# Attention tiles every third step, and vector work moved to the steps that carry attention, in a two-layer encoder on one core

## The chip, the core and the metric

The kernel runs on one core of a Trainium2 chip. A core has five engines with their own instruction queues, which meet through semaphores: TensorE (PE, matrix products), VectorE (DVE), ScalarE (ACT), GpSimd (POOL) and SyncE (SP, which here only issues DMAs). Each engine works its queue strictly in order, so an instruction that waits holds up all that stand behind it. The metric is the device time of one run in microseconds (us), as the median of three.

## The reference

Two layers of a bidirectional encoder over 1024 tokens of width 1024, in float32. Layer 0 has windowed attention with 12 heads over 4 key/value heads; layer 1 has 12 heads, each with three groups of queries (dilations 1, 4 and 16) over the same keys, whose outputs are mixed by their softmax denominators. Both rotate the first 32 of 128 head dimensions, cross-attend with 4 heads into 256 memory tokens, gate, project and normalise.

```python
q, k, v, mq, gate = split_proj(einsum('bld,de->ble', x, w_in), SPLIT)
q, k = apply_rope(q, pos), apply_rope(k, pos)          # first 32 dims of each head
# layer 0: o = softmax over |t-s| <= 128 with a sink logit
# layer 1: for (window, dilation) in ((128,1), (512,4), (2048,16)):
#     o_g, lse_g = band_attention(dilate(q_g), dilate(k), dilate(v))
#   o = sum_g softmax(lse)_g * o_g
y = concat([o_mix, memory_attention(mq, mem, w_mkv)]) * silu(gate)
x = layer_norm(ALPHA * x + y @ w_out, ln_g, ln_b)
```

## The kernel before, in words

The order of all work is written out by hand on a clock of steps, which every engine's program walks through in the same way (`run(layer)` in each engine's block).

**Pairs and steps.** The input projection is done in pairs of 128 output columns: layer 0 has 20 pairs, layer 1 has 40. A pair costs 28 steps (`STEPS`), which are 7 half-size products (a Strassen-like scheme with 7 products in place of 8) of 4 steps each. A step is three matmuls, L1045, L1046 and L1047, of the weights split into a high and a low part. "Step 6 of a pair" below is its seventh step.

**Weights.** Each product takes one stage of weights. SP loads four raw quarters a pair; DVE forms four sums of quarters (`first_sum` to `fourth_sum`); ACT copies the high part (L1261) and DVE subtracts it for the low part (`split_lo`, at steps 2, 6, 10, ... three stages ahead). Nearly all two-operand DVE work goes through the helper `two` and so has the line L1505. The first, second and third sum are made right after `split_lo` of products 0, 1 and 3.

**Results of a pair.** ACT and DVE combine the products in PSUM (`summed`, L1584, on DVE at steps 16, 20 and 24). The one of step 24 (`c11_done`) is what product 0 of the next pair waits for, since it gets the bank.

**Rotary pass.** Each half (512 tokens) of a query or key takes four DVE instructions, one a step (`turn` L1599, `by_cosine`, `by_sine`, `turn_ends`), that start at the steps in `Pair.ropes`: 17 and 25, with two destinations also 21 and 29.

**Attention.** A `Job` is one head (layer 1: one group of a head) with 8 tiles of 128 queries. Tile n of a job that starts at T has its scores on PE at T+2n (L1095, into two banks in turn), its mask with the row minimum on DVE one step later (L1647), the exponential on ACT at +2 (L1339), in layer 0 the normalisation on DVE at +3 (L1653, L1657), the transposes on PE at +5 (L1109), their copy on ACT (L1322), the product with the values on PE at +7 (L1121), and ACT moves each finished half out at +8 (L1368, `output_half`). Scores of tile n wait for the mask of tile n-2, transposes for the exponential.

**Heads of layer 1.** Head i owns pairs 3i (queries of groups 0 and 1), 3i+1 (key and value) and 3i+2 (queries of group 2, and a gate). Its group 0 job runs in pair 3i+2, group 1 in pair 3i+3, group 2 in pair 3i+4, each from step 2. These three are called the g0, g1 and g2 stretches here; in a steady state the three follow each other 12 times. The mixing of head i is timed from T0, the start of pair 3i+5 (a g0 stretch): SP writes the softmax statistics to memory and reads them back token by token from step 0 (L852, L858), DVE works out weights at 11 and 14, SP broadcasts them at 16 to 18 and 29, and DVE multiplies and adds (`mix`, 5 instructions a half) at 26 to 30 and 35 to 39. Steps beyond 27 lie in the next pair, a g1 stretch. The gate product is L1626.

## Time and profile before

| | us |
|---|---|
| three runs | 2269.94, 2273.15, 2278.72; median 2273.15 |
| the profiled execution | 2270.71, span of its instructions 2268.9 |
| PE busy | 2151.3 (95%) |
| weight loads (PEld, beside PE), 11072 of them | 1805.3 (80%) |
| DVE busy | 1629.9 (72%) |
| ACT busy | 1145.5 (50%) |

PE is busy nearly all the time and sets the length; what is not useful in it is idle time and time at the lower of its two clock levels. DVE's 72% is a mean: its work is unevenly spread over the steps. Where matmuls are pipelined, the end of one is modelled, so what a wait costs is read more truly from the distance between starts than from the printed idle time.

### The profile page before, as it was taken

To read this page: it belongs to the slowest core of one execution; us is meant where nothing else is said; L and a number is where in the kernel's file an instruction comes from. 1 tells how busy PE (TensorE), PEld (TensorE's weight loads), DVE (VectorE), ACT (ScalarE), POOL (GpSimd) and SP (SyncE) were. 2 spreads that over 40 slices of the span, in tenths; PEclk is the share of its full clock that TensorE was granted. 3 is DMA by queue.
4 is the path that set the end of the run, shared out by engine and by line. 5 is a ranking of instruction groups with operands and counts; after the bars stand their busy time and mean duration, and the time that the engine had idled before them with its cause. 6 is when DMAs were issued, how large, how long until landed. Compare 5 with 4: busy or idle time off the path is not lost.

```text
span 2268.9 us, 32275 instructions
## 1 busy us (share of the span) xinstructions
PE 2151.3 (95%) x11072; PEld 1805.3 (80%) x11072; DVE 1629.9 (72%) x3673; ACT 1145.5 (50%) x2709; POOL 48.6 (2%) x65
## 2 busy tenths in 40 slices
PE   8999999999999977999999999999999999999996
PEld 8888887878887766887787878877888788888875
DVE  6777777777653759678777777787787777676375
ACT  5454545455543333555555655555556555565332
POOL 0000000000000210000000000000000000000021
PEclk9999999999999988999999999999999999999998
DMA  8311111111147441111212122122121121324743
GB/s 261 92 47 47 56 47 52 54 58 52 47 136 237 131 138 46 59 39 63 66 48 75 53 61 73 37 65 63 48 75 53 61 76 39 93 60 146 236 135 130
DMA packets 206796, 190.34 MB, mean 84 GB/s; under 512 B 20132, under 2 KB 160492, under 8 KB 206636
## 3 DMA queue, kind: packets, MB, share of 16 engines
q1 hardware_dynamic: 206636, 188.29, 26.9%
q8 instruction: 91, 1.49, 0.3%
q14 instruction: 69, 0.57, 0.1%
HBM read 160.01 MB, written 28.23 MB: 83 GB/s over the span
## 4 chain that ended last, share of the span: by engine, by line
PE 64%; DVE 27%; issue 5%; ACT 2%; DMA 2%; SPq 0%; DVEq 0%; ACTq 0%
PE bank L1045 11%; PE bank L1047 11%; PE bank L1046 11%; DVE work L1505 10%; PE bank L1095 7%; PE bank L1121 7%; DVE sums L1505 4%; PE bank L1215 4%; PE bank L1221 4%; PE bank L1109 4%; PE bank L1219 4%; DVE ring L1505 4%; DVE work L1584 2%; DVE work L1599 2%; DVE x_ops L1505 2%
## 5 line engine op out<-in xcount | busy, mean ns | idle before, releaser
L1045 PE MATMUL bank<-x_ops,ring 128*128 128x512 f32 (+1 forms) x1808 | 837.1, 463 | 29.9 <-issue 14.2
L1047 PE MATMUL bank<-x_ops,ring 128*128 128x512 f32 (+1 forms) x1808 | 702.4, 388 | 0.0
L1046 PE MATMUL bank<-x_ops,ring 128*128 128x512 f32 (+1 forms) x1808 | 700.3, 387 | 0.0
L1505 DVE SCALAR_TENSOR_TENSOR ring<-raw,ring 128x512 fp32r<-128x512 f32 x400 | 274.9, 689 | 413.5 <-ACT ring L1261 413.2
L1045 PEld LDWEIGHTS bank<-x_ops,ring 128*128 128x128 f32 x1808 | 347.8, 192 | 90.3 <-issue 43.6
L1047 PEld LDWEIGHTS bank<-x_ops,ring 128*128 128x128 f32 x1808 | 343.3, 190 | 71.6
L1046 PEld LDWEIGHTS bank<-x_ops,ring 128*128 128x128 f32 x1808 | 347.6, 192 | 43.9
L1322 ACT COPY work<-bank 128x256 f32<-128x256 f32 (+2 forms) x448 | 164.0, 366 | 405.2 <-PE bank L1109 403.9
L1261 ACT CAST ring<-raw 128x512 fp32r<-128x512 f32 x400 | 247.8, 621 | 201.1 <-PE bank L1221 172.3
L1095 PE MATMUL bank<-work 128*128 128x256 f32 (+2 forms) x896 | 270.1, 383 | 40.2 <-DVE soft L1647 40.2
L1121 PEld LDWEIGHTS bank<-work 128*128 128x128 f32 x1744 | 263.7, 191 | 43.9 <-ACT work L1368 4.4
L1339 ACT ACTIVATE work<-work,soft 128x256 f32<-128x256 f32 (+2 forms) x448 | 226.7, 506 | 126.1 <-DVE soft L1647 125.4
L1121 PE MATMUL bank<-work 128*128 128x128 f32 x1744 | 267.5, 275 | 3.4 <-ACT work L1368 1.9
L1095 PEld LDWEIGHTS bank<-work 128*128 128x128 f32 x896 | 181.9, 215 | 80.3 <-DVE soft L1647 49.7
L1505 DVE SCALAR_TENSOR_TENSOR work<-work 128x512 f32<-128x512 f32 (+4 forms) x352 | 232.6, 679 | 3.8
L1215 PE MATMUL bank<-ring,x_ops 128*128 128x512 f32 x512 | 200.5, 392 | 8.6 <-DVE x_ops L1505 7.2
L1505 DVE SCALAR_TENSOR_TENSOR work<-work,trig 32x512 f32<-32x512 f32 (+2 forms) x304 | 206.1, 708 | 0.0
L1221 PE MATMUL bank<-ring,x_ops 128*128 128x512 f32 x512 | 199.5, 390 | 0.0
L1219 PE MATMUL bank<-ring,x_ops 128*128 128x512 f32 x512 | 199.5, 390 | 0.0
L1109 PE MATMUL bank<-ident,work 128*128 128x128 f32 x872 | 170.7, 276 | 4.1 <-DVE work L1657 4.0
L1647 DVE CUSTOM_DVE_ANT_0 work<-bank,masks 128x256 f32<-128x256 f32 (+1 forms) x320 | 119.1, 377 | 64.2 <-PE bank L1095 63.0
L1505 DVE SCALAR_TENSOR_TENSOR ring<-sums,ring 128x512 fp32r<-128x512 f32 x180 | 121.0, 672 | 28.9 <-ACT ring L1261 28.9
(75 smaller groups left out, 2125.8 us busy)
## 6 DMA issues: line engine op xcount, KB each, us to landing
raw<-in_w_in_b SPq DMA_DIRECT2D x160, 256.0 KB, 3.0
raw<-in_w_out SPq DMA_DIRECT2D x128, 256.0 KB, 2.9
raw<-in_w_in_a SPq DMA_DIRECT2D x80, 256.0 KB, 3.0
work<-weight_scratch SPq DMA_DIRECT2D x24, 768.0 KB, 5.1
y_scratch<-work SPq DMA_DIRECT2D x32, 512.0 KB, 2.6
x_ops<-y_scratch SPq DMA_DIRECT2D x64, 256.0 KB, 3.8
raw<-in_w_mkv SPq DMA_DIRECT2D x32, 256.0 KB, 5.3
work<-in_x SPq DMA_DIRECT2D x4, 1024.0 KB, 8.1
```

What stands on the lines that cost most here:

```text
L1045: nc.tensor.matmul(dst, w_h, x_h, start=start, stop=False, skip_group_check=again)
L1046: nc.tensor.matmul(dst, w_h, x_l, start=False, stop=False, skip_group_check=again)
L1047: return nc.tensor.matmul(dst, w_l, x_h, start=False, stop=stop, skip_group_check=again)
L1095: nc.tensor.matmul(SB[count % 2][:, 0:size], q, k, start=True, stop=True).then_inc(s_ready, 1)
L1109: mm = nc.tensor.transpose(TB[x_n % 2][:, c * P:(c + 1) * P], p[:, k0:k0 + P], ident[:, :])
L1121: mm = nc.tensor.matmul(dst, job.values(v), pT[layer][count % 2][:, c * P:(c + 1) * P], start=(c == 0), stop=(c == len(chunks) - 1))
L1215: mm = nc.tensor.matmul(BB[b][:, :], y_h, ring[:, n % RING, 0, :], start=first, stop=False)
L1219: nc.tensor.matmul(BB[b][:, :], y_h, ring[:, n % RING, 1, :], start=False, stop=False)
L1221: mm = nc.tensor.matmul(BB[b][:, :], y_l, ring[:, n % RING, 0, :], start=False, stop=last)
L1261: nc.scalar.copy(ring[:, n % RING, 0, :], src).then_inc(w_hi, 1)
L1339: nc.scalar.activation(p_view(layer, count % 3, size, sink), s_view(layer, count % 3, size, sink), ACT.Exp, bias=low[:, job.stat, t:t + 1] ...
L1505: return nc.vector.scalar_tensor_tensor(out=dst, in0=a, scalar=1.0, in1=b, op0=ALU.mult, op1=op)
```

## The change

All of it is in the order of work; no arithmetic changes, and each engine gets the same instructions.

- The jobs of layer 0's 12 heads, and the group 0 and group 2 jobs of layer 1 (but for the last head's group 2), have a tile every third step (`gap=3`) in place of every second. A job then spans steps 2 to 31 of its pair's clock. The group 1 jobs and the memory jobs keep every second step.
- Rotary passes are listed pair by pair. Layer 1: the two queries of pair 3i go to steps 1 to 8 of pair 3i+1 and 1 to 8 of pair 3i+2; the key stays at 17 and 25; the group 2 query goes from 17 and 25 to steps 3 to 10 of the next pair. Layer 0: the keys go to steps 1 to 8 of the next pair, the queries stay.
- The first and third sum of weights are made at steps 3 and 15 of the pair before.
- Mixing is at 25, 27 to 30 and 39 to 43 (before 26 to 30 and 35 to 39), its statistics at step 27 (before 22); outputs, stores and one gate product move some steps later.
- The group 1 and 2 jobs' move-out waits for the mixing of the head before (`mixed`), no longer for its gated output.

```diff
-        ropes = [e for e in range(2) if self.dests[e].rope]
-        if ropes == [0]:
-            self.ropes = [(0, 1, 17), (0, 0, 25)]
-        elif ropes == [0, 1]:
-            self.ropes = [(0, 1, 17), (1, 1, 21), (0, 0, 25), (1, 0, 29)]
...
+        self.ropes = []
...
-            self.gates = [(1, 1, 21, 22), (1, 0, 29, 30)]
+            self.gates = [(1, 1, 21, 27), (1, 0, 29, 30)]
...
+        soon, later = [(0, 1, 17), (0, 0, 25)], [(0, 1, 29), (0, 0, 33)]
...
+            pairs[-1].ropes = later + [(1, 1, 57), (1, 0, 61)]
             add_pair(w_in_b[0], B_K + i * DH, Dest(b_k, "k", order=4), B_V + i * DH, Dest(b_v, "v"))
+            pairs[-1].ropes = soon
...
+            pairs[-1].ropes = [(0, 1, 31), (0, 0, 35)]
...
-            after = [(y_done, 2 * (NE + i))] if i else []
+            after = [(mixed, 10 * i)] if i else []
...
-                          stat=0, needs={0: [ready(pa, 0, 0), ready(pb, 0, 1)],
+                          stat=0, gap=3, needs={0: [ready(pa, 0, 0), ready(pb, 0, 1)],
...
+                          gap=3 if i < HEADS - 1 else 2,
...
-                n, odd = divmod(T - lag - job.start, 2)
+                n, odd = divmod(T - lag - job.start, job.gap)
...
-                if due is not None and due[1] in (0, 1, 3):
-                    {0: first_sum, 1: second_sum, 3: third_sum}[due[1]](due[0])
+                if due is not None and due[1] == 0 and due[0] in FIRST_PAIR:
+                    first_sum(due[0])
+                if due is not None and due[1] == 1:
+                    second_sum(due[0])
...
+                    for when, weight_sum in ((3, first_sum), (15, third_sum)):
...
-                            for h, first in ((0, 26), (1, 35)):
-                                if first <= s < first + 5:
-                                    mix(i, h, s - first)
+                            for h, times in ((0, (25, 27, 28, 29, 30)), (1, (39, 40, 41, 42, 43))):
+                                if s in times:
+                                    mix(i, h, times.index(s))
...
+                    third_sum(FIRST_PAIR[1])
                     fourth_sum(FIRST_PAIR[1])
```

**First place: DVE as a g1 stretch begins.** In both pieces the rows are DVE's from the `split_lo` of step 26 of the g0 stretch on; `ring` is a low part of weights, `raw` and `sums` are sums of weights, L1626 is the gate product and L1647 the mask of a tile (its second row reads out the minimum). Before:

```order
L1505 SCALAR_TENSOR_TENSOR ring<-sums,ring 128x512
L1505 SCALAR_TENSOR_TENSOR work<-work,trig 32x16x32
L1505 SCALAR_TENSOR_TENSOR work<-work 128x512
L1505 SCALAR_TENSOR_TENSOR work<-work,trig 32x512
L1505 SCALAR_TENSOR_TENSOR work<-work 128x512
L1505 SCALAR_TENSOR_TENSOR work<-work 32x16x32
L1505 SCALAR_TENSOR_TENSOR work<-work 128x512 x2
L1505 SCALAR_TENSOR_TENSOR ring<-sums,ring 128x512
L1505 SCALAR_TENSOR_TENSOR raw<-raw 128x512
L1505 SCALAR_TENSOR_TENSOR work<-work 128x512
L1626 SCALAR_TENSOR_TENSOR work<-work 128x512
L1647 ISA work,soft<-bank,masks 128x256
```

Now, from the same `split_lo` (L1517 is the helper's line, L1640 the gate product, L1661 the mask):

```order
L1517 SCALAR_TENSOR_TENSOR ring<-sums,ring 128x512
L1517 SCALAR_TENSOR_TENSOR work<-work 128x512
L1640 SCALAR_TENSOR_TENSOR work<-work 128x512
L1517 SCALAR_TENSOR_TENSOR work<-work 128x512 x2
L1517 SCALAR_TENSOR_TENSOR ring<-sums,ring 128x512
L1517 SCALAR_TENSOR_TENSOR work<-work 128x512
L1640 SCALAR_TENSOR_TENSOR work<-work 128x512
L1517 SCALAR_TENSOR_TENSOR sums<-raw 128x512
L1661 ISA work,soft<-bank,masks 128x256
```

The rotary rows (32 rows high) that stood among the mixing have gone behind the first mask, and a weight sum and a gate product have changed places with others.

**Second place: DVE in the later half of the g1 stretch.** From the `split_lo` of step 14; L1584 (now L1598) combines results of a product, L1599 (now L1613) begins a rotary pass. Before:

```order
L1505 SCALAR_TENSOR_TENSOR ring<-raw,ring 128x512
L1647 ISA work,soft<-bank,masks 128x256
L1647 ISA soft 128x1
L1584 SCALAR_TENSOR_TENSOR work<-bank,work 128x512
L1647 ISA work,soft<-bank,masks 128x256
L1647 ISA soft 128x1
L1599 STREAM_SHUFFLE work<-work 32x512
L1505 SCALAR_TENSOR_TENSOR ring<-raw,ring 128x512
L1505 SCALAR_TENSOR_TENSOR sums<-raw 128x512
L1505 SCALAR_TENSOR_TENSOR work<-work,trig 32x512 x2
L1584 SCALAR_TENSOR_TENSOR work<-bank,work 128x512
L1505 SCALAR_TENSOR_TENSOR work<-work 32x512
```

Now:

```order
L1517 SCALAR_TENSOR_TENSOR ring<-raw,ring 128x512
L1517 SCALAR_TENSOR_TENSOR work<-work 128x512
L1517 SCALAR_TENSOR_TENSOR raw<-raw 128x512
L1661 ISA work,soft<-bank,masks 128x256
L1661 ISA soft 128x1
L1517 SCALAR_TENSOR_TENSOR work<-work 128x512
L1598 SCALAR_TENSOR_TENSOR work<-bank,work 128x512
L1517 SCALAR_TENSOR_TENSOR work<-work 128x512
L1661 ISA work,soft<-bank,masks 128x256
L1661 ISA soft 128x1
L1517 SCALAR_TENSOR_TENSOR ring<-raw,ring 128x512
L1598 SCALAR_TENSOR_TENSOR work<-bank,work 128x512
```

The rotary passes are gone from here; two mixing rows, a weight sum and a gated output have come.

**Third place: PE in a g0 stretch,** two steps before and two after the change (L1109, now L1121, are transposes; L1121, now L1133, products with the values; L1095, now L1107, scores). Before:

```order
L1045 MATMUL bank<-x_ops,ring 128x512
L1046 MATMUL bank<-x_ops,ring 128x512
L1047 MATMUL bank<-x_ops,ring 128x512
L1121 MATMUL bank<-work 128x128 x2
L1109 MATMUL bank<-ident,work 128x128 x2
L1045 MATMUL bank<-x_ops,ring 128x512
L1046 MATMUL bank<-x_ops,ring 128x512
L1047 MATMUL bank<-x_ops,ring 128x512
L1095 MATMUL bank<-work 128x256
```

Now:

```order
L1057 MATMUL bank<-x_ops,ring 128x512
L1058 MATMUL bank<-x_ops,ring 128x512
L1059 MATMUL bank<-x_ops,ring 128x512
L1133 MATMUL bank<-work 128x128 x2
L1057 MATMUL bank<-x_ops,ring 128x512
L1058 MATMUL bank<-x_ops,ring 128x512
L1059 MATMUL bank<-x_ops,ring 128x512
L1121 MATMUL bank<-ident,work 128x128 x2
```

Value products and transposes of different tiles no longer share a step; the scores stand in a third one.

## Rows read from the trace of the kernel before

**Rows 1.** Waits of PE, 870 to 2050 us (total, times, longest).
```profile
PE bank L1095 <- DVE soft L1647: 40.2, 22, 3.0
```
**Rows 2.** By stretch: head 0's g1 stretch (layer 1, pair 3).
```profile
948.60:977.77 29.17, 28.43 (x149) 24.68 (x148) 19.35 (x45) 15.58 (x45) 0.00 (x0) 1.00 0.17 55
```
**Rows 3.** By stretch: two of the eleven other g1 stretches, and the sum of eleven.
```profile
1214.04:1247.97 33.93, 30.21 (x150) 25.69 (x149) 27.41 (x58) 16.39 (x46) 0.00 (x0) 0.95 0.23 71
...
1576.63:1609.26 32.63, 28.91 (x150) 24.77 (x149) 27.33 (x58) 16.52 (x46) 0.00 (x0) 1.00 0.24 73
...
sum 370.18, PE 329.76 PEld 280.60 DVE 297.44 ACT 180.63 POOL 0.31; mean PE 29.98 PEld 25.51 DVE 27.04 ACT 16.42 POOL 0.03
```
**Rows 4.** By stretch: sum of the eleven g2 stretches.
```profile
sum 289.20, PE 279.80 PEld 230.03 DVE 222.52 ACT 157.37 POOL 0.00; mean PE 25.44 PEld 20.91 DVE 20.23 ACT 14.31 POOL 0.00
```
**Rows 5.** PE in order of time, g2 stretch and next start (start, length, what [idle before]).
```profile
1246.83 0.39 PE L1047 MATMUL bank<-x_ops,ring 128*128 128x512 f32 x1
1247.97 0.47 PE L1045 MATMUL bank<-x_ops,ring 128*128 128x512 f32 x1 [0.75 <-DVE work L1584]
...
1253.98 0.40 PE L1047 MATMUL bank<-x_ops,ring 128*128 128x512 f32 x1
1255.07 0.49 PE L1095 MATMUL bank<-work 128*128 128x128 f32 x2 [0.68 <-DVE soft L1647]
...
1274.24 0.47 PE L1045 MATMUL bank<-x_ops,ring 128*128 128x512 f32 x1 [0.17 <-DVE work L1584]
```
**Rows 6.** DVE in order of time: rotary, four full rows, first mask of a g1 stretch.
```profile
1207.58 1.98 DVE L1505 SCALAR_TENSOR_TENSOR work<-work,trig 32x512 f32<-32x512 f32 x2
...
1217.71 2.48 DVE L1505 SCALAR_TENSOR_TENSOR work<-work 128x512 f32<-128x512 f32 x4
...
1222.52 0.41 DVE L1647 CUSTOM_DVE_ANT_0 work<-bank,masks 128x256 f32<-128x256 f32 x1
```
**Rows 7.** PE in order of time: steps with scores, with transposes, with value products.
```profile
1192.36 0.39 PE L1047 MATMUL bank<-x_ops,ring 128*128 128x512 f32 x1
...
1193.27 0.39 PE L1047 MATMUL bank<-x_ops,ring 128*128 128x512 f32 x1
...
1226.35 0.40 PE L1047 MATMUL bank<-x_ops,ring 128*128 128x512 f32 x1
...
1227.50 0.39 PE L1047 MATMUL bank<-x_ops,ring 128*128 128x512 f32 x1
...
1228.85 0.40 PE L1047 MATMUL bank<-x_ops,ring 128*128 128x512 f32 x1
...
1242.96 0.39 PE L1047 MATMUL bank<-x_ops,ring 128*128 128x512 f32 x1
...
1243.64 0.40 PE L1047 MATMUL bank<-x_ops,ring 128*128 128x512 f32 x1
...
1244.79 0.39 PE L1047 MATMUL bank<-x_ops,ring 128*128 128x512 f32 x1
```
**Rows 8.** The start of layer 1: its second pair, and PE's wait before it.
```profile
896.97:918.45 21.48, 21.17 (x85) 16.77 (x85) 18.33 (x42) 5.57 (x10) 0.00 (x0) 0.92 0.17 50
...
PE bank L1045 <- DVE work L1584: 2.2, 1, 2.2
```
**Rows 9.** Waits of PE and of weight loads in layer 0, 126 to 651 us.
```profile
PE bank L1109 <- DVE work L1657: 3.6, 9, 0.4
...
PEld bank L1109 <- DVE work L1657: 8.7, 12, 0.9
```
**Rows 10.** SP in order of time: exchange of softmax statistics, next weight loads.
```profile
1180.80 3.96 SPq L852 DMA_DIRECT2D soft_scratch<-work  x7
1185.85 2.68 SPq L858 DMA_DIRECT2D trig<-soft_scratch  x6
1192.35 0.94 SPq L776 DMA_DIRECT2D raw<-in_w_in_b  x2
```
**Rows 11.** ACT in order of time: a half of a group 1 job moved out.
```profile
1236.86 1.06 ACT L1368 COPY work<-bank 128x256 f32<-128x256 f32 x3
```

More of the change, by code:

```diff
@@ L163, in __init__ @@
     def __init__(self, start, tiles, order, values, out, group=0, sink=None, whole=True, stat=0,
-                 needs=()):
+                 needs=(), gap=2):
+        self.gap = gap
         self.start, self.tiles, self.order, self.values, self.out = start, tiles, order, values, out
@@ L371, in encoder @@
             add_pair(w_in_a[0], A_K + u * DH, k, A_V + u * DH, v)
+            pairs[-1].ropes = later
             for j in range(GROUP):
@@ L391, in encoder @@
                      b_col(1, i), Dest(b_q[1], "q", rot=4 * W_B))
+            pairs[-1].ropes = later + [(1, 1, 57), (1, 0, 61)]
             add_pair(w_in_b[0], B_K + i * DH, Dest(b_k, "k", order=4), B_V + i * DH, Dest(b_v, "v"))
+            pairs[-1].ropes = soon
             q = Dest(b_q[2], "q", order=16)
@@ L427, in encoder @@
                 for e, h, turn in pairs[g].ropes:
+                    assert T0 + turn not in ropes_at[layer]
                     ropes_at[layer][T0 + turn] = (g, e, h)
-                    rope_no[g, e, h] = len(rope_no)
                 for e, h, tanh, mul in pairs[g].gates:
@@ L432, in encoder @@
                     gate_no[g, e, h] = len(gate_no)
+            for T in sorted(ropes_at[layer]):
+                rope_no[ropes_at[layer][T]] = len(rope_no)
         def landed(g, e, h):
@@ L514, in encoder @@
                               order=A_ORDER, values=chunks_of(a_vbuf), out=a_o[j], sink=h,
-                              stat=h % 3,
+                              stat=h % 3, gap=3,
                               needs={0: [ready(gk, 0, 0), ready(gq, 0, 1)], 4: [ready(gq, 0, 0)]})
@@ L598, in encoder, with stat_time @@
         tile_no, x_no, y_no, job_no = {}, {}, {}, 0
-        stats_at = {step_at(1, 3 * i + 4, 22): i for i in range(HEADS)}
+        def stat_time(i):
+            return step_at(1, 3 * i + 4, 27 if i < HEADS - 1 else 22)
+        stats_at = {stat_time(i): i for i in range(HEADS)}
         y_at = ({}, {})
@@ L652, in x_of_tile @@
         def x_of_tile(layer, job, n):
-            return x_no[layer, job.start + 2 * n + LAG_T, "tile"]
+            return x_no[layer, job.start + job.gap * n + LAG_T, "tile"]
         def products(layer):
@@ L1766, in run @@
                         fourth_sum(pair.g + 1)
+                    for when, weight_sum in ((3, first_sum), (15, third_sum)):
+                        pair = pair_at(layer, T, when)
+                        if pair is not None and pair.g + 1 < FIRST_PAIR[layer] + PAIRS[layer]:
+                            weight_sum(pair.g + 1)
                     for job in jobs[layer]:
```

11 lines of the change are left out of this document (5 added, 6 removed).

## The prediction

> **What bounds the kernel now.** I read the page's busy shares first: PE 95%, DVE 72%, ACT 50%. PE sets the length, so only three things can move the time: how long PE stands, how long it runs at the lower clock level, and how its own instructions follow each other. Next I read who PE waits for. In layer 1's projection the scores wait 22 times for the mask on DVE [rows 1], twice for each of eleven heads. Then I laid windows on the pairs. A g1 stretch with nothing in its way takes 29.17 us; that is head 0's, which no mixing precedes [rows 2]. The eleven others take 32.6 to 34.2 us with the same matmuls, and the longer ones show a mean granted clock of 0.95, the shorter 1.00 [rows 3]. So behind a stand of some 3 us PE sometimes runs on at 1.2 GHz for a while. The window with the lower clock is 1.3 to 1.6 us longer than the one without.
>
> Last I read what DVE did before such a stand. In the stretch that begins at 1214.04 us, the first mask belongs to step 3 and starts at 1222.52, 8.5 us after the stretch began [rows 6]. DVE was never idle there: it was late, because steps 17 to 30 of the g0 stretch held two rotary passes, three combinations, weight sums, gate and mixing, while PE went through the steps after the last tile at only 0.68 us each (1242.96 to 1243.64) [rows 7]. A full-size DVE instruction costs 0.61 us (four in 2.48), a strided rotary product 0.99 (two in 1.98) [rows 6]. Each step without attention hides one DVE instruction, and these steps held more.
>
> **Prices on PE.** All prices are distances between starts of the third matmul of two steps [rows 7]: a bare step 0.68, with scores 1.15 (1226.35 to 1227.50), with value products and transposes together 1.35 (to 1228.85), with transposes alone 0.91 (1192.36 to 1193.27), with value products alone 1.15 (1243.64 to 1244.79).
>
> **Part 1: the g1 stretch.** Its tiles keep their spacing; what goes is the work ahead of them. I tallied DVE against PE from the start of the stretch. Up to the first mask DVE now has six full instructions (three mixing, one low part, one gate, one weight sum), 3.7 us; the mask needs the scores of step 2, which PE has done at 3.2. So the mask is done at about 4.1 us, against 8.9 before. Two strided rotary passes follow at steps 3 to 10, of 3.2 us each (begin and end 0.61, two products 0.99), among masks (0.35), low parts, output and the second mixing. By that tally masks 0 to 7 are done at 4.1, 6.4, 9.5, 11.6, 14.1, 15.7, 18.4 and 20.6 us. PE asks for the transposes of those tiles at 6.9, 9.0, 11.5, 14.0, 16.5, 19.0, 21.0 and 23.0. With 0.7 us for the exponential between, each is in time by 1.2 us or more. Hence no stand, and with it no lower clock. Gain: 370.18 - 11 x 29.17 = 49.3 us [rows 2, 3]. What is late next is ACT: at step 16 it waits for the last mixing instruction of step 15 (formerly for the output of step 12), done at some 19.0 us while PE enters step 16 at 17.7. Behind it in ACT's queue stand three copies of 1.06 us [rows 11] and the copy of transposed tile 5, which PE wants at 21. Between 0 and 1.3 us per head; I take 0.3, x 11 = 3 us lost.
>
> **Part 2: the g2 stretch.** Two stands, both visible as distances [rows 5]. At its first step, 1246.83 to 1247.97 is 1.14 where 0.23 is usual, so 0.91 lost: the combination of step 24 of the g1 stretch was late, behind rotary passes that are now elsewhere. At its first masks, 1253.98 to 1255.07 is 1.09, so 0.86 lost, for the pass that ran over from steps 25 and 29. Gain 11 x 1.77 = 19.5 us; the stretch's mean falls from 26.3 [rows 4] to 24.5. The new load here is the densest of the change: from step 16 to the combination of step 24, seven full instructions, one strided pass and two small masks make 8.1 us. PE wants that combination at step 28, at 24.5/28 = 0.88 us a step 10.5 us after step 16. It fits with 2.4 us to spare. DVE then enters the g0 stretch about 2 us late and has two more passes there, but now beside tiles; the tally has its first mask done at 5.2 us and PE asking for the transposes at 7.8.
>
> **Part 3: the g0 stretch.** The stand at its first step (0.17 idle shown, 0.33 by the same difference between shown and true as at the g2 start) has the same cause as the 0.91: 11 x 0.33 = 3.6 us. The end of this stretch, which made DVE late before, now holds 11 full instructions and four masks in steps 16 to 27, 8.1 us, over some 12 us of PE.
>
> **Part 4: the start of layer 1.** PE stands 2.2 to 2.4 us for the first pair's combination and then has a pair at clock 0.92 [rows 8]; seven of DVE's instructions ahead of that combination move off. I take 2.4 and 1.7 for the clock (0.08 of 21.48). Gain 4.1 us. Third sum of weights now before the last normalisations at the layer's end: one instruction, on the path there, costs 0.6.
>
> **Part 5: layer 0.** Transposes wait for DVE: 3.6 us idle on PE, 8.7 on the weight loads [rows 9]. These two bound it; with one instruction's start hidden under each I take 6.6 us. The rotary passes and tiles here tally at about DVE's full rate in steps 16 to 27 (14.7 us against 14.4), late by 1 us at most, which the four steps of slack hide.
>
> **Part 6: what PE pays.** 280 tiles (96 in layer 0, 96 + 88 in layer 1) now leave the product stream three times, not twice. Apart: 0.91 + 1.15 - 0.68 = 1.38; together 1.35 [rows 7]. The rows are rounded to 0.01, so 0.01 to 0.04 a tile, 3 to 11 us; I take 5.
>
> The Trainium skill ("TensorE: Matmul & The Clock Gate", section "Back-to-back issue gap") says that in a real stream the spacing of matmuls is set by weight load and matmul both, so that small matmuls leave a load uncovered. By that rule every new return to the product stream would show a load. These rows do not bear it out: the lone transposes add 0.23, barely over two of their starts. It stands below as a rival.
>
> **Parts with one answer.** Later outputs, stores and gates, and the memory jobs: nothing waits for them in the stretches above, the next reader of each buffer being a stretch or more away. If that cover went, each would cost its own 0.6 us once a head.
>
> **Sum,** against the profiled execution's 2270.71 (span 2268.9): 49.3 + 19.5 + 3.6 + 4.1 + 6.6 = 83.1 gained; 5 + 3 + 0.6 = 8.6 paid; 74.5 net, 2196.2. That execution lies 2.4 under the median 2273.15; I add 2 for that: 2198 us.
>
> **Rivals.**
> A. The backlog moves and does not go. For: DVE is near its full rate at the end of g2 and at the start of g1, with margins of 1.2 to 2.4 us, and one late semaphore uses them up. Against: the tallies. Price: 1.5 us in each of 12 heads and the full 1.3 on ACT in 11: 18 + 11 = 29 more: 2227.
> B. PE's switching. Every new return shows a whole weight load. For: the weight loads are busy 80% of the span. Against: [rows 7]. A load takes 0.163 us in the mean (1805.3 over 11072 loads, by the page): 280 x 0.163 = 46, 5 of it counted: 2239. This is the skill's rule above, as this kernel would show it.
> C. Slower. The statistics leave at step 27, not 22, so SP's exchange runs inside the g0 stretch. From its first write at 1180.80 to the last read issued at 1188.53 is 7.7 us, and 1.1 more if the reads land as the last write did (issued by 1184.76, waited out at 1185.85): 8.8 us [rows 10]. DVE needs it at step 11, at 29.17/28 = 1.04 us a step 11.5 us in, less half a step until the statistics are there: 2.2 us spare. If the exchange takes longer, DVE stands with all masks behind it, and SP's weight loads too. It decides from 75/12 = 6.2 us a head, an exchange of over 17 us; at 18 it gives 2280. For: the exchange will share the queues with weight loads. Against: nothing in the rows is nearly so slow.
> D. It does not do what it says: the waits put down to DVE are another's, and the time stays at 2270. Against: the 8.5 us without one idle moment on DVE.
>
> **How the numbers follow.** Forecast 0.78, A 0.13, B 0.03, C 0.03, D 0.03. 0.5% (11 us) is about what can be told from no change. Faster: forecast, A and B, 0.94; same: D, 0.03; slower: C, 0.03. Range: downward, nothing paid at ACT, 3 on PE and 8.7 in layer 0, then a few us for waits in the last heads that I left out: 2184. Upward, to A: 2226.
>
> **What would show it.** PE's waits for DVE at the scores go from 40.2 us to under 5; the eleven g1 stretches sum to 321 to 326, the g2 stretches to about 271; no clock below 1.00 between 910 us and the end of layer 1's projection; PE busy nearly unchanged in the g0 stretches. If part 1 is wrong, scores or transposes in g1 still wait for DVE, or value products for ACT at steps 17 to 21. If C holds, DVE waits for a DMA at its first copy of weights (L1671). The prediction is wrong if the product stream itself lengthens by over 0.05 us a tile.

## The result, and the profile after

The changed kernel takes 2181.57 us (median of four runs, 2181.03 to 2183.19) against 2271.55 us for the kernel before beside it: a ratio of 0.9598, 95% interval 0.9581 to 0.9616. The profiled execution took 2181.57 us, its span is 2179.8, which is 89.1 us under the span before. So the kernel is 4% faster, as forecast in sign and for the most part in cause, but the forecast of 2198 us was 16.4 us too high and the range ended 2.4 us above the result.

Of the page, first the busy shares, and then the first line on the chain of waits:

```profile
PE 2121.7 (97%) x11072; PEld 1787.8 (82%) x11072; DVE 1628.8 (75%) x3673; ACT 1139.9 (52%) x2709; POOL 48.6 (2%) x65
...
PE 91%; DVE 5%; issue 1%; DMA 1%; ACT 1%; SPq 0%; ACTq 0%; DVEq 0%
```

The chain of waits was 64% PE and 27% DVE before. DVE did the same work (1629.9 us before, 1628.8 after); only its times moved. PE's busy time fell by 29.6 us with the same matmuls.

The waits of PE from 860 to 1985 us (total, times, longest), which answer to [rows 1]:

```profile
PE bank L1133 <- ACT work L1334: 1.2, 2, 0.7
PE bank L1133 <- ACT work L1380: 0.7, 1, 0.7
PE bank L1121 <- DVE work L1671: 0.5, 1, 0.5
PE bank L1036 <- DVE x_ops L1517: 0.2, 1, 0.2
```

The 40.2 us at the scores (now L1107) are gone. By stretch, the windows that answer to [rows 3] (the same two heads, and the sum of the eleven g1 stretches), and to [rows 4] (sum of the g2 stretches):

```profile
1184.30:1213.50 29.20, 29.20 (x157) 25.51 (x156) 26.51 (x57) 16.84 (x47) 0.00 (x0) 1.00 0.25 82
...
1518.33:1547.56 29.23, 29.23 (x157) 25.52 (x156) 26.52 (x57) 16.84 (x47) 0.00 (x0) 1.00 0.25 82
...
sum 321.38, PE 321.38 PEld 280.67 DVE 291.65 ACT 185.20 POOL 0.31; mean PE 29.22 PEld 25.52 DVE 26.51 ACT 16.84 POOL 0.03
...
sum 269.79, PE 269.79 PEld 225.00 DVE 211.05 ACT 145.43 POOL 0.00; mean PE 24.53 PEld 20.45 DVE 19.19 ACT 13.22 POOL 0.00
```

PE is busy through the whole of each g1 window, at clock 1.00. At the g2 start, which answers to [rows 5], PE in order of time (start, length):

```profile
1213.28 0.39 PE L1059 MATMUL bank<-x_ops,ring 128*128 128x512 f32 x1
1213.50 0.39 PE L1057 MATMUL bank<-x_ops,ring 128*128 128x512 f32 x1
```

That is 0.22 between starts, where it was 1.14. And of DVE, for [rows 6], the low part of weights of step 26 and the first mask of the g1 stretch that began at 1184.30:

```profile
1184.15 0.69 DVE L1517 SCALAR_TENSOR_TENSOR ring<-sums,ring 128x512 fp32r<-128x512 f32 x1 [2.25 <-ACT ring L1273]
...
1189.58 0.42 DVE L1661 CUSTOM_DVE_ANT_0 work<-bank,masks 128x256 f32<-128x256 f32 x1
```

The mask starts 5.3 us into the stretch; before it was 8.5. The tally of the prediction had it done at 4.1, and it is done at about 5.7. DVE is not late by a backlog here: it stood idle for 2.25 us until ACT had copied the high part, and so began step 26's low part only as the stretch began. Nine full instructions, that one included, stand ahead of the mask, where the tally counted six.

The two layers as wholes, from the first matmul of the first pair to that of the last step. Before, then after (us, PE busy, weight loads, DVE, ACT, POOL, granted clock, DMA share, GB/s):

```profile
73.76:651.48 577.72, 572.61 (x2953) 473.82 (x2951) 420.28 (x1048) 286.93 (x676) 0.00 (x0) 1.00 0.17 54
856.85:2068.57 1211.72, 1153.74 (x6021) 974.18 (x6022) 926.53 (x2220) 682.55 (x1731) 0.31 (x1) 0.98 0.21 60
```

```profile
72.96:643.74 570.78, 570.30 (x2952) 471.58 (x2951) 420.72 (x1048) 283.92 (x676) 0.00 (x0) 1.00 0.18 55
849.03:1980.51 1131.48, 1127.11 (x6021) 959.36 (x6022) 924.37 (x2219) 679.78 (x1731) 0.31 (x1) 1.00 0.22 65
```

Layer 0 gained 6.9 us and layer 1 gained 80.2; the other 1.9 lie outside the projections, where the change moves nothing on PE.

### The profile page after: what moved, and what is told of

Its sections match the earlier page's. It is cut to its first block, busy times and chain, and to the rows that moved or that the text cites. A ratio compares the mean times of both kernels' runs of the same rounds, so it can differ in the third digit from the quotient of the medians.

```text
span 2179.8 us, 32275 instructions
## 1 busy us (share of the span) xinstructions
PE 2121.7 (97%) x11072; PEld 1787.8 (82%) x11072; DVE 1628.8 (75%) x3673; ACT 1139.9 (52%) x2709; POOL 48.6 (2%) x65
## 4 chain that ended last, share of the span: by engine, by line
PE 91%; DVE 5%; issue 1%; DMA 1%; ACT 1%; SPq 0%; ACTq 0%; DVEq 0%
PE bank L1059 18%; PE bank L1057 18%; PE bank L1058 18%; PE bank L1133 9%; PE bank L1107 9%; PE bank L1121 4%; PE bank L1227 4%; PE bank L1233 4%; PE bank L1231 4%; PE bank L1097 2%; DVE x_ops L1517 1%; DVE work L1517 1%; PE bank L1036 1%; DVE ring L1517 1%; DMA raw<-in_w_mkv 1%
## 5 line engine op out<-in xcount | busy, mean ns | idle before, releaser
L1058 PE MATMUL bank<-x_ops,ring 128*128 128x512 f32 (+1 forms) x1808 | 696.9, 385 | 0.0
L1517 DVE SCALAR_TENSOR_TENSOR ring<-raw,ring 128x512 fp32r<-128x512 f32 x400 | 273.0, 684 | 240.8 <-ACT ring L1273 240.6
L1058 PEld LDWEIGHTS bank<-x_ops,ring 128*128 128x128 f32 x1808 | 345.3, 191 | 36.5
L1133 PEld LDWEIGHTS bank<-work 128*128 128x128 f32 x1744 | 262.2, 190 | 44.5 <-ACT work L1334 3.7
L1133 PE MATMUL bank<-work 128*128 128x128 f32 x1744 | 267.3, 274 | 2.5 <-ACT work L1334 1.2
L1107 PE MATMUL bank<-work 128*128 128x256 f32 (+2 forms) x896 | 264.4, 376 | 0.0
L1517 DVE SCALAR_TENSOR_TENSOR work<-work 128x512 f32<-128x512 f32 (+4 forms) x352 | 233.3, 678 | 4.1 <-DMA work<-weight_scratch 0.9
L1517 DVE SCALAR_TENSOR_TENSOR ring<-sums,ring 128x512 fp32r<-128x512 f32 x180 | 123.1, 684 | 114.5 <-ACT ring L1273 114.5
L1517 DVE SCALAR_TENSOR_TENSOR work<-work,trig 32x512 f32<-32x512 f32 x304 | 207.1, 710 | 0.8
L1107 PEld LDWEIGHTS bank<-work 128*128 128x128 f32 x896 | 181.6, 215 | 30.2
L1121 PE MATMUL bank<-ident,work 128*128 128x128 f32 x872 | 168.2, 272 | 0.5 <-DVE work L1671 0.5
L1121 PEld LDWEIGHTS bank<-ident,work 128*128 128x128 f32 x872 | 114.4, 140 | 33.2 <-ACT work L1351 2.5
```

The lines of the kernel that those rows point to most:

```text
L1058: nc.tensor.matmul(dst, w_h, x_l, start=False, stop=False, skip_group_check=again)
L1107: nc.tensor.matmul(SB[count % 2][:, 0:size], q, k, start=True, stop=True).then_inc(s_ready, 1)
L1121: mm = nc.tensor.transpose(TB[x_n % 2][:, c * P:(c + 1) * P], p[:, k0:k0 + P], ident[:, :])
L1133: mm = nc.tensor.matmul(dst, job.values(v), pT[layer][count % 2][:, c * P:(c + 1) * P], start=(c == 0), stop=(c == len(chunks) - 1))
L1517: return nc.vector.scalar_tensor_tensor(out=dst, in0=a, scalar=1.0, in1=b, op0=ALU.mult, op1=op)
```

## The experiments

Each ran on the chip beside the kernel before; ratios are to that, with their 95% interval. "Changed kernel" is the kernel of the result, and edits are against that one unless said otherwise. A stand is a stretch of time in which PE waits. Line numbers shift by a few with some edits.

### 1. Rotary passes and weight sums at their old places (e1), rotary passes alone (e3)

```
 e3:      self.ropes = []           ->  passes at steps 17, 25 (and 21, 29)
          pairs[-1].ropes = later   ->  deleted, as the other four such lines
 e1: as e3, and first_sum and third_sum back at their old places
```

Both keep the new spacing, and also the new places of mixing, gates, statistics and outputs.

> The changed kernel with the rotary passes and the weight sums back at their old steps; tile spacing, mixing, gates and statistics stay at the new ones. Theory 1 (the gain comes from DVE work taken out of the steps ahead of a g1 stretch; spacing only makes room for it): about half of the 89 us is kept. The stand at the start of g2 (0.9) and at its masks (0.9) stays, the stand of 3.4 in g1 shrinks to about 2, the clock seldom falls: about 2225 us, 2215 to 2240. Rival 2 (the spacing alone gives the time, since it keeps PE slower and fed while DVE catches up): 2182 to 2190. Rival 3 (only the moves count): 2265 to 2275.

> The changed kernel with the rotary passes alone back at their old steps; the weight sums stay at 3 and 15. Theory 1: near the first experiment, better by the one weight sum (0.6 us) that no longer stands ahead of the first mask of g1 and one in steps 17 to 24: 2210 to 2225. Rival 2: 2182 to 2190. If the sums carry the gain: below 2195.

Measured: e1 2244.59 us, 0.9875 (0.9854 to 0.9895); e3 2246.05, 0.9877 (0.9852 to 0.9903). Both keep under a third of the gain, and both are slower than their first theory had it (2215 to 2240 for e1, 2210 to 2225 for e3). The scores of the g1 stretches stand for DVE again. Shown are the waits of PE from 860 to 1985 us in e1 (L1108 are the scores; L1058 is the first matmul of a step, which waits for the combination of step 24; L1122 are transposes, which wait for the exponential), then two of its eleven g1 stretches with their sum, and the same sum for e3:

```profile
PE bank L1108 <- DVE soft L1660: 27.3, 11, 2.5
PE bank L1058 <- DVE work L1597: 11.2, 13, 2.2
PE bank L1122 <- ACT work L1352: 5.9, 11, 0.6
```

```profile
1025.70:1058.64 32.94, 29.73 (x158) 25.45 (x156) 27.65 (x59) 18.23 (x52) 0.00 (x0) 1.00 0.22 72
1113.85:1148.14 34.29, 31.06 (x157) 26.38 (x156) 27.66 (x59) 18.12 (x52) 0.00 (x0) 0.95 0.21 70
...
sum 367.29, PE 332.09 PEld 283.88 DVE 300.40 ACT 199.70 POOL 0.31; mean PE 30.19 PEld 25.81 DVE 27.31 ACT 18.15 POOL 0.03
...
sum 369.33, PE 337.94 PEld 288.01 DVE 301.12 ACT 198.59 POOL 0.32; mean PE 30.72 PEld 26.18 DVE 27.37 ACT 18.05 POOL 0.03
```

So part 1 of the prediction named the right work: with the rotary passes alone where they were (e3), 47.9 of the 48.8 us of the g1 stretches come back. Part 2 is borne out by half: of the 19.4 us of the g2 stretches 9.9 come back in e3 and 10.6 in e1, as a stand at their first step and one at the transposes. Two things did not follow. Layer 0 stayed as in the changed kernel in both runs, to 0.1 us a pair, so the move of the rotary passes is not needed for its gain. And the g0 stretches kept their 29.76 us: the stand at their start, which part 3 put down to the rotary passes, stays away without them having moved.

### 2. The moves without the new spacing (e2)

```
-                n, odd = divmod(T - lag - job.start, job.gap)
+                n, odd = divmod(T - lag - job.start, 2)
```

The same 2 stands for `job.gap` in `x_of_tile`.

> The changed kernel with a tile every second step in all jobs; rotary passes, sums, mixing, gates and statistics stay at the new steps. Theory 1: the moved rotary passes are what matters; at the end of g0 DVE has 6.7 us of work in steps 16 to 27 against 8.2 us of PE, so the g1 stretches have no stand; g2 ends with DVE 2.5 us late, and small stands of up to 1 us a head appear in g0: 2185 to 2200. Rival 2 (spacing is needed): above 2220. Theory on PE's order: if the third leaving of the product stream costs 0.02 us a tile, 280 tiles give 5 us back here, and this kernel ties with the changed one.

Measured: 2195.68 us, 0.966 (0.964 to 0.968), within the expected 2185 to 2200. Layer 1 as a whole, and PE's waits in it:

```profile
848.77:1993.92 1145.15, 1131.62 (x6021) 965.91 (x6022) 923.70 (x2219) 681.28 (x1731) 0.31 (x1) 1.00 0.22 64
...
PE bank L1107 <- DVE soft L1661: 9.2, 22, 0.6
```

The scores stand twice per g1 stretch, 22 times, but briefly; no g1 stretch shows a lower clock. With the moves in place, the spacing is thus worth 1145.15 - 1131.48 = 13.7 us in layer 1. The g1 jobs have the same spacing in both kernels. What differs is the stretch before: in e2, DVE begins the low part of step 26 at 0.58 us into the g1 stretch that starts at 1186.93 (here too after a wait for ACT's copy), not 0.15 ahead of it, and PE would reach the scores of the third tile at 5.7 us, not at 6.65. The gains of the parts do not add up: e1 keeps 25 us and e2 76 us of the 89, by the spans 2243.7 and 2193.2.

### 3. The weight sums at their old places (e4)

```
-                if due is not None and due[1] == 0 and due[0] in FIRST_PAIR:
-                    first_sum(due[0])
+                if due is not None and due[1] in (0, 1, 3):
+                    {0: first_sum, 1: second_sum, 3: third_sum}[due[1]](due[0])
```

> The changed kernel with the first and third weight sum alone back behind split_lo of products 0 and 3. Theory 1: the third sum comes ahead of the first mask of g1 in place of the first sum, same count there; one more instruction in steps 17 to 24 of each pair uses 0.6 of the 2.4 us to spare in g2: 2182 to 2190. If DVE's margins are already used up in the changed kernel: 2200 or more, with stands for the combination of step 24 at the starts of g0 and of layer 0's pairs.

Measured: 2182.88, 0.9603 (0.9584 to 0.9623). This is within the expected 2182 to 2190. Moving the sums is worth nothing that can be told, and costs nothing that can be told.

### 4. One break fewer per tile (f1)

```
+    def lag(self, lag):
+        return lag + (self.gap == 3 and lag in (7, 8))
...
-            fills[1][T0 + 3] = ([(c22_done, pb + 1)], tiles_v[4:8], b_vbuf[0], HALF)
-            fills[1][T0 + 4] = ([(c21_done, pb + 1)], tiles_v[0:4], b_vbuf[0], 0)
+            fills[1][T0 + 3] = ([(c21_done, pb + 1)], tiles_v[0:4], b_vbuf[0], 0)
+            fills[1][T0 + 4] = ([(c21_done, pb + 1)], tiles_v[4:8], b_vbuf[0], HALF)
```

The second piece makes two fills of the value buffer, in layer 1, change places; so f1 is not the one edit alone there.

> The changed kernel, but in the jobs with a tile every third step the value products come one step later (8 steps behind the scores, moving out at 9), so that they share a step with the transposes of the next tile and PE leaves the product stream twice a tile, not three times. Theory 1 (a further return to the stream costs 0.012 to 0.018 us, by the difference of the changed kernel and e2_moves_only in layer 0 and in stretches without their stands): 280 tiles, 3.4 to 5 us less than the changed kernel, 2177 us. Rival (the returns cost nothing, and the payment in the prediction was no cost at all): 2181 to 2182. Rival (a whole weight load shown each time, 0.16): 2137.

Measured: 2185.68, 0.9635 (0.9622 to 0.9648), and a span of 2183.9, 4.1 above the changed kernel's, 1.4 of it a fall of the clock in layer 1's first pair. One g0, g1 and g2 stretch of it, with their sum:

```profile
1155.36:1185.24 29.88, 29.84 (x161) 25.38 (x160) 23.79 (x60) 20.85 (x46) 0.00 (x0) 1.00 0.26 64
1185.24:1214.84 29.60, 29.60 (x159) 25.85 (x158) 26.68 (x57) 17.17 (x48) 0.00 (x0) 1.00 0.27 81
1214.84:1239.17 24.33, 24.33 (x131) 20.36 (x129) 19.20 (x51) 13.01 (x38) 0.00 (x0) 1.00 0.15 45
sum 83.81, PE 83.77 PEld 71.58 DVE 69.66 ACT 51.03 POOL 0.00; mean PE 27.92 PEld 23.86 DVE 23.22 ACT 17.01 POOL 0.00
```

The same three take 83.47 us in the changed kernel (29.74, 29.20, 24.53). The g2 stretch wins 0.2; the last value products of the g0 job now fall into g1, which loses 0.4. The expected 2177 was missed, and so were both rivals (2181 to 2182, and 2137). In layer 0, where the fills are as they were, the time from the first pair's start to the twentieth's is 542.86 us, against 543.22 in the changed kernel: 0.4 saved over 96 tiles. So putting two of three breaks together saves next to nothing there, and nothing in layer 1. Why g0 does not shrink by what g1 takes on was not followed up.

### 5. How near the next waits are (f2, f3, f4)

f2 gives ACT its old, later release; f3 and f4 make the weight sum of step 3 two and four more times, ahead of the first mask of each of the eleven g1 stretches. The values that the kernel computes stay the same.

```
 f2: -            after = [(mixed, 10 * i)] if i else []
     +            after = [(y_done, 2 * (NE + i))] if i else []
 f3: +                if g - 1 >= FIRST_PAIR[1] + 6 and (g - 1 - FIRST_PAIR[1]) % 3 == 0:
     +                    for _ in range(2):
     +                        two(sums[:, 0], quarter(g, 0), quarter(g, 1), ALU.add).then_inc(again, 1)
     ...
 f4: as f3, with range(4)
```

> The changed kernel with the move-out of the group 1 and group 2 jobs waiting again for the head's gated output, not for its mixing. In a g1 stretch of the changed kernel ACT starts those three copies right after the last mixing instruction, and its copy of tile 5 is done some 0.2 us before PE wants it. Theory 1 (ACT's hold is real, and only just hidden): the output stands two DVE instructions later (1.2 us), so PE stands about 1.0 us a head, 11 us in all: 2190 to 2195. Rival (ACT has room, the hold was never near PE): 2181 to 2184.

> The changed kernel with the weight sum of step 3 made two more times (each waiting for the one before, 0.7 us each) in the eleven g1 stretches from pair 6 on: 1.4 us more on DVE ahead of the first mask. Theory 1 (what binds is the scores, which wait for the mask two tiles back; in the changed kernel they have only 0.3 us to spare at tile 4): PE stands 1.1 to 1.4 us a head, 12 to 15 us in all: 2193 to 2197. Rival, the prediction's own tally (the transposes bind, 1.2 us to spare): 0.2 us a head, 2182 to 2185.

> As before with four more, 2.8 us ahead of the first mask. Theory 1: 2.5 us a head, 27 us in all, a little more for what a stand costs beyond its own length: 2208 to 2212; if stands of this length bring the lower clock, 1.7 us for each time it comes, up to 2228. Rival, the prediction's tally: 1.6 a head, 2199. It also tells how long a stand has to be for the clock to fall: the stands of e1_spacing_only at 2.6 us were followed by it in four of eleven stretches.

Measured: f2 2196.30, 0.9681 (0.9668 to 0.9695); f3 2200.42, 0.9701 (0.9688 to 0.9714); f4 2218.70, 0.9782 (0.9768 to 0.9795). PE's waits for the engine concerned, in f2, f3 and f4:

```profile
PE bank L1133 <- ACT work L1334: 10.1, 11, 0.9
```

```profile
PE bank L1109 <- DVE soft L1668: 7.0, 22, 0.4
```

```profile
PE bank L1109 <- DVE soft L1668: 22.0, 18, 1.9
```

In f2 each g1 stretch grows by 1.15 us (30.36 to 30.39): ACT's copies of the finished outputs come too late, and the value products behind them stand. So the hold at ACT is real (the median is 1.3 above the expected 2190 to 2195), and the changed kernel is only just past it. There the copy of tile 5 ends at 1206.04, 0.15 ahead of the value products that need it:

```profile
1205.62 0.42 ACT L1334 COPY work<-bank 128x256 f32<-128x256 f32 x1
...
1206.19 0.62 PE L1133 MATMUL bank<-work 128*128 128x128 f32 x4
```

In f3 it is the scores that stand, not the transposes, which the prediction's tally had as next. The scores of tile 2 need the mask of tile 0: in the changed kernel they start at 1190.95, with that mask done at about 1190.00, so 0.95 us spare. Those of tile 4 have least; they need the mask of tile 2, whose minimum is read out by 1195.2, 0.3 ahead of them:

```profile
1194.78 0.41 DVE L1661 CUSTOM_DVE_ANT_0 work<-bank,masks 128x256 f32<-128x256 f32 x1
...
1195.51 0.61 PE L1107 MATMUL bank<-work 128*128 128x256 f32 x2
```

Both are under the 1.2 that the prediction gave the transposes as the least. The 22 stands of f3 are these two in each stretch, and f4's repeats add 1.45 us more to the first. The times lie above the expected 2193 to 2197 in f3 and between 2208 and 2228 in f4, nowhere near the rival's 2182 to 2185 and 2199.

f3 shows too what a stand costs besides its length. PE in order of time at step 6 of a g1 stretch, first the changed kernel, then f3:

```profile
1190.72 0.40 PE L1059 MATMUL bank<-x_ops,ring 128*128 128x512 f32 x1
1190.95 0.61 PE L1107 MATMUL bank<-work 128*128 128x256 f32 x2
1191.21 0.58 PE L1057 MATMUL bank<-x_ops,ring 128*128 128x512 f32 x1
```

```profile
1196.06 0.39 PE L1061 MATMUL bank<-x_ops,ring 128*128 128x512 f32 x1
1196.85 0.84 PE L1109 MATMUL bank<-work 128*128 128x256 f32 x2 [0.40 <-DVE soft L1668]
1197.34 0.58 PE L1059 MATMUL bank<-x_ops,ring 128*128 128x512 f32 x1
```

The idle time shown is 0.40. The start of the scores is 0.79 behind the last product, not 0.23: 0.56 lost. From the scores to the next product it is 0.49, not 0.26: another 0.23, since the second of the two score matmuls follows the first by 0.44 and not by 0.22. One stand of "0.40" costs 0.79.

In f4 the same stand is 2.0 us by starts. In four of the eleven stretches the clock falls after it, in seven not (two neighbours):

```profile
1278.16:1310.23 32.07, 29.99 (x157) 25.51 (x156) 29.24 (x61) 16.84 (x47) 0.00 (x0) 1.00 0.26 74
1364.53:1397.52 32.99, 31.13 (x157) 26.69 (x156) 29.24 (x61) 17.27 (x47) 0.00 (x0) 0.95 0.23 72
```

### 6. Where layer 0's gain comes from (g1, g2, g3, h1, h2)

g1 is the changed kernel once more. g2 puts layer 0's tiles back to every second step; g3 besides puts back its rotary passes; h1 besides the weight sums, which leaves of the change only the later outputs in layer 0, and the first gate product of a pair at step 27, not 22, which no run puts back; h2 is g3 with the outputs back, so that only the sums and that gate product are moved there. Layer 1 keeps the change in all of them (in h1 but for the sums).

```
 g2: -                              stat=h % 3, gap=3,
     +                              stat=h % 3, gap=2,
 g3: -            pairs[-1].ropes = later
     +            pairs[-1].ropes = [(0, 1, 17), (0, 0, 25)]
 h2: -  add_outcome(0, h, a_o[j], a_gate, gp, 1, T0 + 35, T0 + 36, T0 + 37, f"o{j}")
     +  add_outcome(0, h, a_o[j], a_gate, gp, 1, T0 + 31, T0 + 32, T0 + 33, f"o{j}")
```

> The changed kernel once more, as the partner of the next two on the same chip. Its profiled span was 2179.8 us and its ratio to the kernel before 0.960. Theory 1 (its gain is a property of its order): 0.960 within 0.002, layer 0's groups of three attended pairs take 31.6, 31.5 and 31.5 us again, and the eleven g1 stretches 29.2 each. Theory 2 (the first pair of layer 1 differs between executions by chance, by one fall of the clock): pair 0 takes either 36.1 or about 37.5 us in it, and nothing else moves.

> The changed kernel with the tiles of layer 0 every second step again, while rotary passes and sums stay where the change put them, in both layers; layer 1 keeps its third-step tiles. Theory 1 (in layer 0 the moves alone take the stands away, and a third return to the product stream costs a tile 0.01 us): about 0.7 us less than the changed kernel in the span, layer 0 only, 2181 or so in the median; that cannot be told in medians, but in the windows. Theory 2 (layer 0 needs the spacing): its attended pairs grow back by 0.5 us each, 12 x 0.5 = 6 us, 2188.

> As the run before it (layer 0's tiles every second step), and in layer 0 the rotary passes back at steps 17 and 25 of the key pairs too, so that of the change layer 0 keeps only the moved weight sums and the later outputs; layer 1 keeps all. It asks why layer 0 gained over 8 us although old rotary places with the new spacing lost nothing there. Theory 1 (either of the two, spacing or rotary places, is enough in layer 0, and without both the transposes stand for DVE): the stands come back, 0.5 to 0.7 us in each of twelve attended pairs, 7 us, median 2188. Theory 2 (the later outputs and moved sums alone free layer 0): no stand, the time of the run before it, 2181.

> Layer 0 as in the run before (tiles every second step, rotary passes of all pairs at steps 17 and 25), and besides the weight sums back where they stood, in both layers; of the change layer 0 keeps only its later outputs (steps 35 and 36, not 31 and 32). That run had no stand in layer 0, so the later outputs or the moved sums alone free it. Theory 1 (it is the sums: the first sum stood ahead of the last tile's normalisation, at step 19, and held it): the stands come back, some 0.5 us in each of twelve attended pairs, 6 to 7 us, 2188. Theory 2 (it is the outputs): no stand, attended pairs of 32.3, 31.4 and 31.4 us again, 2182.

> The mirror of the run before: layer 0 with tiles every second step, rotary passes at steps 17 and 25, outputs back at steps 31 and 32, and only the weight sums moved. Theory 1 (sums): no stand, 2182, attended pairs of 32.3, 31.4 and 31.4 us. Theory 2 (outputs): the stands come back, 6 to 7 us, 2188. If neither of the two runs has the stands, either edit alone is enough, and the stand in the kernel before needed both to be as they were.

Measured: g1 2183.63, 0.9625 (0.9604 to 0.9645); g2 2182.09, 0.9618 (0.9598 to 0.9639); g3 2181.70, 0.9615 (0.9595 to 0.9635); h1 2180.87, 0.9612 (0.9596 to 0.9628); h2 2187.80, 0.9638 (0.9623 to 0.9652). g1's ratio is just above the 0.960 within 0.002 that was expected. Layer 0 as a whole in g2, g3, h1 and h2, and at the end PE's wait in h2 from 115 to 580 us:

```profile
72.63:642.14 569.51, 569.03 (x2953) 475.12 (x2951) 420.94 (x1048) 286.42 (x676) 0.00 (x0) 1.00 0.18 55
```

```profile
72.92:642.39 569.47, 568.99 (x2953) 475.10 (x2951) 420.62 (x1048) 286.40 (x676) 0.00 (x0) 1.00 0.18 55
```

```profile
73.23:642.82 569.59, 569.11 (x2952) 474.74 (x2951) 420.15 (x1048) 286.95 (x676) 0.00 (x0) 1.00 0.18 55
```

```profile
72.67:648.75 576.08, 571.49 (x2953) 474.26 (x2951) 420.54 (x1048) 287.46 (x676) 0.00 (x0) 1.00 0.17 54
...
PE bank L1121 <- DVE work L1671: 4.0, 8, 0.5
```

I had expected g3 to bring the stands back; it did not. Only h2 does, with the wait of [rows 9]. Layer 0 gains by its later outputs: 576.08 - 569.47 = 6.6 us, and neither by spacing nor by rotary places. Another 1.6 us (577.72 - 576.08) go with something else; 1.0 of it lies in the three pairs without attention in the middle of layer 0, which take 19.38 us before and 19.04 in both h1 and h2. Whether sums, outputs or the gate product free these is open. The mechanism of the 6.6 stands in DVE's order. Before, at steps 3 to 5 of an attended pair, and the same place in h1:

```profile
265.46 0.60 DVE L1647 CUSTOM_DVE_ANT_0 work<-bank,masks,sinks_neg 128x384 f32<-128x384 f32 x1
265.99 0.07 DVE L1647 DVE_READ_ACCUMULATOR2_ANT soft<- 128x1 f32 x1
265.99 1.27 DVE L1728 SCALAR_TENSOR_TENSOR work<-work 128x512 f32<-128x512 f32 x2
267.20 0.60 DVE L1647 CUSTOM_DVE_ANT_0 work<-bank,masks,sinks_neg 128x384 f32<-128x384 f32 x1
...
267.92 0.42 DVE L1657 TENSOR_SCALAR work<-work,zinv 128x384 f32<-128x384 f32 x1
```

```profile
263.01 0.60 DVE L1659 CUSTOM_DVE_ANT_0 work<-bank,masks,sinks_neg 128x384 f32<-128x384 f32 x1
...
263.55 0.60 DVE L1659 CUSTOM_DVE_ANT_0 work<-bank,masks,sinks_neg 128x384 f32<-128x384 f32 x1
...
264.59 0.42 DVE L1669 TENSOR_SCALAR work<-work,zinv 128x384 f32<-128x384 f32 x1
```

Two gated outputs (L1728) stood between the first mask and that tile's normalisation (L1657), for which the transposes wait. From mask to normalisation it was 2.46 us and is 1.58.

g2 also prices the third-step order of tiles with its third return to the product stream: 570.78 - 569.51 = 1.27 us over 96 tiles, 0.013 us each. f1 takes away the third return alone and gets back under a third of that, so the return's own share is smaller. With layer 0 at every second step the kernel is no faster by its medians; h1's span, 2178.0, is the shortest of all, 1.8 under the changed kernel's and 3.8 under g1's, which differ by 2.0 between themselves. No version was found that is faster than the changed kernel by more than that.

Tiles at every third step in the group 1 jobs as well were not tried: by the order of the code the last tiles' scores would read queries that are being overwritten by then.

## Why the prediction was right, and where it failed

The sign, the main cause and most of the confirming signs of the prediction came in: no wait at the scores, g1 sum 321.38 (321 to 326 said), g2 sum 269.79 (about 271), clock 1.00 from 910 us on to the end of the projection. PE's busy time in the g0 stretches, said to be nearly unchanged, fell by 0.44 of 30.19 us each. Its size was 14.6 us short in the span (89.1 against 74.5), and the 2 us added for the median belonged to the execution before alone, since the profiled execution after lies on its median.

| | forecast, net | measured | missed |
|---|---|---|---|
| the eleven g1 stretches (part 1, less 3 at ACT) | 46.3 | 370.18 - 321.38 = 48.8 | 2.5 |
| g2, g0 and head 0's g0 stretch (parts 2, 3; less 3.3 of part 6) | 19.8 | 19.4 + 4.8 + 0.8 = 25.0 | 5.2 |
| start of layer 1 (part 4) | 3.5 | 6.2 | 2.7 |
| layer 0 (part 5; less 1.7 of part 6) | 4.9 | 6.9 | 2.0 |
| outside the stretches named | 0 | 2.2 | 2.2 |

Three steps failed, in that they sized a term wrongly, and none of them alone makes up the 14.6. The first two lines are to be read together, since with tiles every third step the tail of a g0 job runs on into the g1 stretch. By the tallies above, their 7.7 us are 3.0 at ACT that were not paid, 3.2 of the next paragraph, 0.8 in head 0, and 0.7 of roundings and of part 6.

**Two signs came in by luck.** Part 1 called head 0's g1 stretch one with nothing in its way. It is not: of its 29.17 us PE is busy for 28.43 [rows 2], and the rest is the stand at the first step of the next stretch, since a window runs to the first matmul behind it. Clean, the same stretch takes 28.27, as in e2, where no tail of another job runs into it:

```profile
934.16:962.43 28.27, 28.27 (x149) 24.82 (x148) 19.29 (x44) 14.93 (x43) 0.00 (x0) 1.00 0.18 57
```

In the changed kernel it takes 29.18 again, because the last tile of the g0 job, spaced wider, now ends in it. So the 0.91 that left at one end came in at the other, and the g1 sum lay in its range. The g2 mean of 24.5 was likewise got by taking the 0.91 off a window that does not hold it; what the window lost in its place is the stand at the g0 start, the whole price of the one at the masks, and its own last tile (24.83 in e2, 24.53 in the changed kernel). Nothing is counted twice, and the sum over the three stretches holds: before, 90.14 us a head; after, 83.50.

**Step that failed: the price of a stand.** Parts 2 and 3 took the late first start alone: 0.91, 0.86 and 0.33. The whole steps lose more. From 1246.83 to the third matmul of the next step is 1.68 us by [rows 5] and the rows between, where 0.68 is bare: 1.00. Likewise 0.97 for the 0.86 and 0.42 for the 0.33, together 0.29 a head, 3.2 us in all. f3 shows such a second loss by itself, 0.23 behind a stand of 0.56.

**Step that failed: what is late next.** Part 1 charged ACT 3 us. The hold is real, as f2 shows, but the changed kernel clears it by 0.15 us: its copies start at 1204.74 as soon as mixing is done, and PE has no idle time in the g1 windows. Its lower bound, nothing, held. On DVE's side the least margin lay at the scores, with 0.3 us; the prediction's tally did not look at them. The tally of the masks was 1.4 to 1.6 us too early for all eight, as it left out the three instructions that wait behind ACT's copy at step 26. It had PE's transposes too early as well, by 0.9 to 1.4, as it left out the g0 job's tail. The two errors cancel, so that the transposes had their margin of over 1.2 us by luck too.

**Step that failed: "nothing waits" for the later outputs.** They were put with the parts that have one answer, at nothing. In layer 0 they are most of the gain, 6.6 us (g3 against h2). That part 5 also has 6.6, for the stands in layer 0 by other edits, is chance. All that left layer 0 was worth 577.72 - 569.51 = 8.2, near the 8.7 of the weight loads' wait [rows 9], which was the truer bound. 1.3 of it goes to the wider spacing.

**Part 3's cause is not borne out:** in e3 the g0 start does not stand though the rotary passes are back. Nor does it in e2, with the old spacing. Either of the two may be enough by itself, or it is the gates, mixing or outputs, which no run undoes in layer 1; this stays open.

**Part 4** took one fall of the clock at the start of layer 1. There were two, one in the second pair [rows 8] and one in the first, whose window shows a mean clock of 0.91 before and 0.94 after; both kernels also enter it at the lower level from the work between the layers. Its first pair gained 4.0 us and its second 2.2. This place is not steady: g1, the same kernel, took 37.5 us in the first pair, not 36.1, with one more fall there.

**Part 6 was right in size:** 280 tiles at 5 us. By layer 0 it is 0.013 a tile. In layer 1, e2's g0, g1 and g2 without their stands of 1.6 us make 83.2 against 83.47, some 0.017 a tile over 16; together an estimated 4.4 us. It is the price of the wider spacing; f1 does not show it to be the third return's.

**The range.** Its lower end, 2184, already took nothing at ACT and 8.7 us in layer 0, and a few us for the last heads. These last did not come: the three pairs behind the eleventh g1 stretch of the sum take 99.0 us, and took 99.3. That 2184 was missed by only 2.4 us is owed to them; what it lacked are the second loss behind the stands, the start of layer 1 and what lies outside.

**The rivals.** A would have shown as waits at scores or transposes; there are none in the three stretches. B's price was 0.163 us a tile, and the runs show a tenth of that. The section "Back-to-back issue gap" of the Trainium skill's page "TensorE: Matmul & The Clock Gate" says that in a real stream weight load and matmul together set the spacing. Read as rival B reads it, each return would show its weight load; the 0.013 us a tile do not bear that reading out. C's wait of DVE for a DMA at the weights' first copy is not in the trace (DVE waits for one once, 0.9 us, at head 0's mixing); the third sum ahead of the last normalisations cost nothing either, since the stretch between the layers changed by 0.1 us. D fell.

**Left over:** 2.2 us outside the named stretches, of which 0.8 are before layer 0 and 1.1 behind layer 1, where both kernels do the same; g1 against the result moved by 2.0 in the span as well.

## What to carry to other kernels

Price a stand by the whole step or the whole stretch against a clean one, never by the idle time shown nor by the first late start. When an in-order engine is the one waited for, read what stands in its queue between two instructions of the same tile: two outputs of no urgency there cost layer 0 6.6 us. Before a window is taken as clean, look whether PE is busy to its very end. And before an edit is put at nothing, undo it alone, since edits made together hide whose the gain is.

## What the runs showed of the hardware

- After a stand of 2.0 us (f4) the granted clock fell in four of eleven stretches that hold the same instructions, after one of 2.6 us (e1) likewise in some and not in others; after stands of 0.56 (f3) and 1.09 us (f2) in none of the eleven. A fall cost 0.9 us in f4 and about 1.3 in e1.
- Behind a stand ahead of two small matmuls the second comes late too, by 0.23 us (f3, after 0.56, and f4, after 2.0), which no idle time shows.
- A tile at every third step, with three returns to a stream of 512-column matmuls and not two, costs 0.013 us more (g2), though the weight loads are busy for 82% of the span.
